# Routing the last token tile from un-normalised values, with logits corrected by mean and deviation

## The reference

```
mixed = merged @ w_out
x = LN1(alpha * x + mixed)               # (v - mean) * rsqrt(var + eps) * g + b
group = argmax(x @ w_rg)                 # 4 groups
two experts of that group by x @ w_re    # 32 experts in all
moe = sum over the two of weight * (silu(x @ w1[e]) * (x @ w3[e])) @ w2[e]
ple = sigmoid(x @ w_ple_gate) * (p @ w_ple)
x = LN2(alpha * x + moe + ple)
```

## Time and profile before

| | |
|---|---|
| runs | 1535.27, 1535.79, 1536.26 us, median 1535.79 |
| profiled execution | 1533.7 us, span 1531.9 us, mean granted clock of PE 0.932 |
| PE busy | 1288.9 us, 84% |
| DVE, ACT, POOL busy | 404.1, 284.8, 54.0 us |
| data moved | 488.77 MB, mean 319 GB/s |
| border from mixing to experts | 303 to 317 us in layer 0, 1055 to 1069 us in layer 1 |

### The profile page before, as it was taken

How to read it: one execution, slowest core, us unless ns; L and a number is a source line. 1 busy time by engine, 2 the same in 40 slices (tenths; PEclk the granted TensorE clock), 3 DMA queues, 4 the chain that set the end, 5 groups by cost and what they waited for, 6 DMA issues and landing times.

```text
span 1531.9 us, 20304 instructions
## 1 busy us (share of the span) xinstructions
PE 1288.9 (84%) x8528; PEld 718.5 (47%) x8529; DVE 404.1 (26%) x1027; ACT 284.8 (19%) x712; POOL 54.0 (4%) x94
## 2 busy tenths in 40 slices
PE   7999999999788777755799999999997786776754
PEld 4766887544332332321276678766442331332311
DVE  4142633532111101100133446245211211101003
ACT  3342422021001101000034434212111101010001
POOL 1300000000000000000022010000000000000000
PEclk9999999999898978988999999999998998888887
DMA  9503435999999999999962042579999999999994
GB/s 332 163 1 110 172 117 180 417 363 426 427 427 426 426 427 426 427 426 426 407 217 84 32 149 102 181 268 372 403 427 427 426 426 427 427 426 427 426 426 162
DMA packets 99534, 488.77 MB, mean 319 GB/s; under 512 B 9520, under 2 KB 15600, under 8 KB 51952
## 3 DMA queue, kind: packets, MB, share of 16 engines
q1 hardware_dynamic: 94976, 476.48, 76.2%
q0 software_dynamic: 4464, 10.93, 2.4%
HBM read 484.48 MB, written 2.89 MB: 318 GB/s over the span
## 4 chain that ended last, share of the span: by engine, by line
PE 58%; DMA 33%; SPq 6%; DVE 2%; issue 1%; ACT 0%; POOL 0%; DVEq 0%
PE bank L1002 55%; DMA arena<-in_w_e_up 12%; DMA arena<-in_w_e_down 8%; DMA ring<-in_w_e_down 5%; DMA arena<-in_w_e_gate 3%; SPq L791 3%; SPq L857 2%; DMA xT<-in_w_e_down 2%; PE bank L1052 2%; DMA ring<-in_w_e_gate 2%; DMA ring<-in_w_in 1%; DVE arena L2007 0%; DVE x_sb L2016 0%; PE bank L1447 0%; DVE arena L2119 0%
## 5 line engine op out<-in xcount | busy, mean ns | idle before, releaser
L1002 PE MATMUL bank<-arena 128*32 128x512 f32 (+13 forms) x2840 | 546.9, 537 | 101.5 <-DMA arena<-in_w_e_down 22.8
L1002 PE MATMUL bank<-ring,arena 128*32 128x512 f32 (+4 forms) x1248 | 398.2, 645 | 38.0 <-issue 16.0
L1002 PEld LDWEIGHTS bank<-arena 128*32 128x32 f32 (+4 forms) x2840 | 199.5, 136 | 307.2 <-issue 298.7
L1002 PE MATMUL bank<-ring,xT 128*32 128x128 f32 (+5 forms) x1536 | 236.5, 363 | 1.3 <-ACT xT L1608 1.1
L1002 PE MATMUL bank<-xT,ring 128*128 128x288 f32 x768 | 191.8, 407 | 0.0
L1002 PEld LDWEIGHTS bank<-ring,xT 128*32 128x32 f32 (+1 forms) x1536 | 121.1, 137 | 100.3 <-issue 89.6
L1002 PEld LDWEIGHTS bank<-xT,ring 128*128 128x128 f32 x768 | 143.7, 190 | 37.9
L1002 PEld LDWEIGHTS bank<-ring,arena 128*32 128x32 f32 (+1 forms) x1248 | 97.9, 130 | 107.6 <-issue 93.9
L1002 PE MATMUL bank<-arena,x_sb 128*128 128x128 f32 (+1 forms) x768 | 99.7, 282 | 1.4 <-DVE arena L2339 0.8
L1002 PEld LDWEIGHTS bank<-arena,x_sb 128*128 128x128 f32 (+1 forms) x768 | 90.5, 190 | 19.5 <-issue 12.7
L1002 PE MATMUL bank<-lb,arena 128*32 128x512 f32 x128 | 73.6, 729 | 28.3 <-DMA arena<-in_w_e_up 28.3
(11 more groups left out here) (234 smaller groups left out, 892.5 us busy)
## 6 DMA issues: line engine op xcount, KB each, us to landing
arena<-in_w_e_gate SPq DMA_DIRECT2D x76, 1024.0 KB, 25.6
arena<-in_w_e_up SPq DMA_DIRECT2D x70, 1024.0 KB, 26.2
arena<-in_w_e_down SPq DMA_DIRECT2D x60, 1024.0 KB, 26.2
ring<-in_w_e_up SPq DMA_DIRECT2D x42, 1024.0 KB, 26.3
ring<-in_w_e_gate SPq DMA_DIRECT2D x38, 1024.0 KB, 26.3
ring<-in_w_e_down SPq DMA_DIRECT2D x38, 1024.0 KB, 26.2
ring<-in_w_in SPq DMA_DIRECT2D x32, 1024.0 KB, 10.0
lb<-in_w_e_up SPq DMA_DIRECT2D x12, 1024.0 KB, 26.5
```

What stands on the lines that cost most here:

```text
L1002: return pe.matmul(out, lhsT, rhs, start=first, stop=last, skip_group_check=True)
```

## The change

Tile 1 is no longer routed from LN1's result. Its residual sums are transposed as they are (`turn_raw`, one half of the features as soon as its sum is written) and multiplied with `wr_scaled`, the router columns times LN1's g. The logits come out of three terms: with s the raw product, m the mean and r the inverse deviation of a token, they are r * (s - m * sum(g w)) + sum(b w). The two sums over features are 16 products with one-column weights (`router_sums`; g and b by columns are the new input `ln1_cols`), copied to SBUF by ACT and spread over 128 partitions by one product (`spread_sums`). LN1 of tile 1 still runs, partly beside the routing; its second half is shifted after `place_tile(1)`. The normalised tile is transposed into `xT` in quad 0, behind the choice's transposition. `plain(0, 2)` moves from the border to quad 0, behind `plain(1, 2)`. `gather_first((2, 0))` now stands behind `router(1)`.

```diff
-            (("rk", 2), 4), (("rk", 0), 5), (("wo", 1, 1), 2), (("t1", 1, 0), 0), (("t1", 1, 1), 1), (("rt", 1), 3),
-            (("pl", 0, 2), 2), (("pg", 0, 2), 5), (("rk", 1), 4), (("XT0", 0), 6), (("XT0", 1), 7), (("cnt",), 3)]
+            (("rk", 2), 4), (("rk", 0), 5), (("raw", 0), 0), (("wo", 1, 1), 2), (("sw",), 7), (("raw", 1), 1), (("sb",), 7), (("rt", 1), 3),
+            (("rk", 1), 4), (("XT0", 0), 6), (("XT0", 1), 7), (("cnt",), 3)]
...
+    turned = [(("t1", 1, 0), 5), (("t1", 1, 1), 6)]
+    j = [(("G",), 0)] + ([(("ST0",), 4)] + turned if g == 0 else [])
...
+    j += [(("Y", 0), 5), (("Y", 1), 6)] + (plain(1, 2, 1, 2) + plain(0, 2, 7, 0) if g == 0 else []) + combine
...
+        norm_cols = carve(5568, 2, 8)
+        wr_scaled = carve(5584, 8, 36)
...
                 pool.dma_start(pT[:, :, SEQ:T], p_sample[layer]).then_inc(ple_in, 16)
+                pool.dma_start(norm_cols, ln1_cols[layer].rearrange("p (k c) -> p k c", k=2)).then_inc(norm_cols_in, 16)
...
-                            job_read(pe, (layer, "t1", t, c // 4))
+                            job_read(pe, (layer, "raw", c // 4) if t == 1 else (layer, "t1", t, c // 4))
+                        ins = mm(b[0:NT[t], 0:36], xT[:, c, now(t)], (wr_scaled if t == 1 else wr)[:, c, :], c == 0, c == 7)
...
+                def turn_raw(h):
+                    pe.wait_ge(x_mixed, 2 * layer + h + 1)
+                    transposes(layer, ("raw", h), [((c % 4) * P, P, x[0:P, 1, c * P:c * P + P]) for c in range(4 * h, 4 * h + 4)])
+                def router_sums():
+                    pe.wait_ge(norm_cols_in, 16 * (layer + 1))
+                    b = open_bank((layer, "sw"))
+                    for k in range(2):
+                        for c in range(8):
+                            ins = mm(b[0:1, 36 * k:36 * k + 36], norm_cols[:, k, c:c + 1], wr[:, c, :], k + c == 0, c == 7)
+                    done(ins)
+                def spread_sums():
+                    job_read(pe, (layer, "sw"))
+                    b = open_bank((layer, "sb"))
+                    done(mm(b[:, 0:72], ones[0:1, :], wr_sums[0:1, :], True, True))
...
                 rank(0)
+                turn_raw(0)
                 half_mix(1, 1)
+                router_sums()
+                turn_raw(1)
+                spread_sums()
+                pe.wait_ge(wr_scaled_out, layer + 1)
+                router(1)
                 pe.wait_ge(sel_early, layer + 1)
                 gather_first((2, 0))
-                turn_mixed(1)
-                router(1)
                 pe.wait_ge(ple_in, 32 * (layer + 1))
-                plain(0, 2)
                 rank(1)
...
                         transpose_choice((layer, "ST0"))
+                        turn_mixed(1)
...
                         plain(1, 2)
+                        plain(0, 2)
...
+                read_raw(0)
+                act.activation(wr_sums[0:1, 0:36], bank(key)[0:1, 0:36], ACT.Copy, scale=-1.0)
+                emptied(act.copy(wr_sums[0:1, 36:72], bank(key)[0:1, 36:72]), key)
+                read_raw(1)
+                layer_norm(1 + 2 * layer, (1,))
+                emptied(act.copy(wr_sums_all, bank(key)[:, 0:72]), key)
...
+                    if t == 1:
+                        job_read(dve, (layer, "sb"))
+                        dve.wait_ge(ln_rstd, ln_place(1 + 2 * layer, t))
+                        step(dve.scalar_tensor_tensor(raw_logits, wr_sums_all[:, 0:36], mvs[:, 2:3], b[:, 0:36], ALU.mult, ALU.add))
+                        step(dve.scalar_tensor_tensor(raw_logits, raw_logits, ln_rs[:, 1:2], wr_sums_all[:, 36:72], ALU.mult, ALU.add))
...
+                dve.tensor_tensor(wr_scaled, wr, bcast(norm_cols[:, 0, :], 2, 36), ALU.mult).then_inc(wr_scaled_out, 1)
...
-                normalize(1 + 2 * layer, 1, x[:, 1, :], x_half)
-                read_x("t1", layer, xT, (1,))
+                job_done(dve, (layer, "raw", 1))
+                for h in range(2):
+                    half = x[:, 1, 512 * h:512 * h + 512]
+                    ins = dve.scalar_tensor_tensor(half, half, mvs[:, 2:3], lnw[:, 0, 512 * h:512 * h + 512], ALU.subtract, ALU.mult)
+                step(ins)
                 route_tile(1)
+                shift_half(0).then_inc(x_half, 1)
                 place_tile(1).then_inc(sel_out, 1)
+                shift_half(1).then_inc(ln_out, 1)
...
-                gated(0, 2)
...
+                        read_x("t1", layer, xT, (1,))
...
                         gated(1, 2)
+                        gated(0, 2)
```

More of the change, by code:

```diff
@@ L279, in __init__ @@
                 for job, b in expert_jobs(g):
-                    enter((layer,) + job if job[0] in ("pl", "pg", "ST0") else (layer, "moe", g) + job, b)
+                    enter((layer,) + job if job[0] in ("t1", "pl", "pg", "ST0") else (layer, "moe", g) + job, b)
     def number(self, key):
@@ L604, in build @@
         ln_rows_out = sem("ln_rows_out")
+        norm_cols_in = sem("norm_cols_in")
+        wr_scaled_out = sem("wr_scaled_out")
+        x_mixed = sem("x_mixed")
         rows_in = sem("rows_in")
@@ L1322, in router @@
                         if c % 4 == 0:
-                            job_read(pe, (layer, "t1", t, c // 4))
-                        ins = mm(b[0:NT[t], 0:36], xT[:, c, T0[t]:T0[t] + NT[t]], wr[:, c, :], c == 0, c == 7)
+                            job_read(pe, (layer, "raw", c // 4) if t == 1 else (layer, "t1", t, c // 4))
+                        ins = mm(b[0:NT[t], 0:36], xT[:, c, now(t)], (wr_scaled if t == 1 else wr)[:, c, :], c == 0, c == 7)
                     done(ins)
+                def turn_raw(h):
[12 more added lines that the diff above has]
+                    done(mm(b[:, 0:72], ones[0:1, :], wr_sums[0:1, :], True, True))
                 def turn_mixed(t):
                     for h in range(2):
[L1330 to L1333, removed]
+                        pe.wait_ge(ln_out, ln_place(2 * layer + 1, t))
                         transposes(layer, ("t1", t, h), [((c % 4) * P, P, x[0:NT[t], t, c * P:c * P + P]) for c in range(4 * h, 4 * h + 4)])
@@ L1375, in gather_first @@
                         for t in tiles:
+                            if t == 1 and h == 0:
+                                pe.wait_ge(x_half, 2 * layer + 2)
+                            elif t == 1:
+                                pe.wait_ge(ln_out, ln_place(2 * layer + 1, t))
                             for c in range(4):
@@ L1528, in _ @@
                     if g == 0:
+                        for h in range(2):
+                            job_read(pe, (layer, "t1", 1, h))
                         plain(0, 1)
@@ L1873, in plain_gate, with read_raw @@
                     emptied(act.activation(sums(layer, t, j), for_sums(layer, t, bank(key)), ACT.Sigmoid), key)
-                for t in MIX_ORDER:
-                    layer_norm(1 + 2 * layer, (t,))
-                    read_x("t1", layer, t, (0, 1) if t != 1 else (0,))
+                def read_raw(h):
+                    key = (layer, "raw", h)
+                    job_done(act, key)
+                    emptied(act.copy(xT[:, 4 * h:4 * h + 4, now(1)], transposed(bank(key), 1)), key)
+                for t in (2, 0):
+                    layer_norm(1 + 2 * layer, (t,))
+                    read_x("t1", layer, t, (0, 1))
+                read_raw(0)
+                key = (layer, "sw")
+                job_done(act, key)
+                act.activation(wr_sums[0:1, 0:36], bank(key)[0:1, 0:36], ACT.Copy, scale=-1.0)
+                emptied(act.copy(wr_sums[0:1, 36:72], bank(key)[0:1, 36:72]), key)
+                read_raw(1)
+                layer_norm(1 + 2 * layer, (1,))
+                key = (layer, "sb")
+                job_done(act, key)
+                emptied(act.copy(wr_sums_all, bank(key)[:, 0:72]), key)
                 for t in MIX_ORDER:
@@ L1940, in _ @@
                         read_choice((layer, "ST0"))
+                        read_x("t1", layer, 1, (0,))
                         plain_gate(0, 1)
@@ L1951, in _ @@
                         plain_gate(1, 2)
+                        plain_gate(0, 2)
                         read_tokens((layer, "moe", g, "XT", 0))
@@ L2320, in route_tile @@
                     step(dve.tensor_scalar(r[:, 48:52], iota[0:n, 0:4], r[:, 16:17], 2 * BIG, ALU.is_equal, ALU.mult))
[L2321 to L2324, removed]
+                    ins = dve.scalar_tensor_tensor(lg[:, 8:40].rearrange("p (g e) -> p g e", g=GROUPS), bcast(r[:, 48:52], 2, PER_GROUP),
+                                                   BIG, b[0:n, 4:36].rearrange("p (g e) -> p g e", g=GROUPS),
+                                                   ALU.subtract, ALU.min)
+                    if t == 1:
+                        step(ins)
+                    else:
+                        emptied(ins, key)
+                        job_read(dve, key)
                     step(dve.max(r[:, 24:32], lg[:, 8:40]))
@@ L2347, in place_tile @@
                     return ins
```

(18 more changed lines are left out.)

14 lines of the change are left out of this document (10 added, 4 removed).

## The result

The changed kernel takes 1542.2 us in the median of 22 runs (1530.35 to 1547.24); the kernel before takes 1535.33 beside it (22 runs, 1533.69 to 1538.27). It is slower: the medians differ by 6.9 us, the means by 5.2, because the changed kernel's runs are spread over 17 us with some short ones among them. The recorded ratio is 1.0034, with an interval of 1.0019 to 1.0049. The forecast was 1533.2, with a range of 1530.3 to 1536.0, and no rival that I named gives this time for the reason that holds.

A forecast was written before the change was run, and what follows sets the result against it. The expert weight stream was taken to bound the kernel, stalling once per layer at the mixing-to-experts border. Experts 1.3 us sooner in 2 layers save 2.6: profiled 1533.7 becomes 1531.1, median 2.1 above, 1533.2 us; range 1530.3 to 1536.0.

The forecast's parts named there:

- PE is at its higher level throughout: At the border from mixing to experts, TensorE was taken to run at granted clock 1.00, 2.4 GHz.
- so layer 0 is worked out and doubled: Layer 1 was said to run layer 0's sequence, so its 1.3 us saving was counted twice: 2.6 us.
- The sums: `router_sums` on PE after the last `wo` half: 16 matmuls, 32 records, 1.55 us, bounds 1.28 and 1.87.
- the spread row: `spread_sums` before `router(1)`: 0.35 us waiting for ACT's copy, an estimate between 0 and 0.7, plus 0.1 for the matmul.
- `gather_first`, not routing, is last: Behind `router(1)`, `gather_first((2, 0))` holds PE until 312.1, 1.0 us later than routing's 311.1.
- The two corrections: Two small DVE operations turning raw logits into logits: 0.45 us with hand-over, costing nothing because `gather_first` ends later.
- The one gap of PE: Sign of a correct forecast: between the last `wo` half and the experts, PE has no gap over 0.3 us.
- The shift's second half: LN1's second half, behind `place_tile(1)`, lasts until 314.3; the gather wants it at 314.4, late by 0.2 at worst.
- The correction costs what it saves: Rival: sums, spread row and late second half add up at the border; 1.3 us longer erases the gain, 1535.8; chance 0.13.
- a warm restart: Rival: blocks follow the `lnw` piece without a stream start-up, up to 1.5 us more a layer, 1530.2; chance 0.20.
- Quad 0 starves the stream: Rival: PE's later release in quad 0 is paid if under 2.6 us of transfers lie ahead: 1541.0; chance 0.07.
- `plain(0, 2)` leaves PE, where it stood in the shadow of routing, so its removal saves nothing: At the border, moving these products to quad 0 was priced at zero; in quad 0 they take 2.30 us.

The follow-up runs named there:

- again: The changed kernel run once more with no edit, to profile an execution of usual length: 1542.64 us, ratio 1.0053.
- plain_back: The changed kernel with `plain(0, 2)` put back at the border, ahead of `rank(1)`, new routing kept: 1544.59 us, ratio 1.006.
- move_only: The kernel before with only `plain(0, 2)` moved from the border to quad 0, LN1 and routing unchanged: 1538.97 us, ratio 1.0019.
- thick: The changed kernel plus two unread dense 512-column products, one behind `router(1)`, one behind `gather_first((2, 0))`: 1536.41 us, ratio 1.0003.
- thick_small: The changed kernel plus two unread dense products of 128 columns, behind `router(1)` and behind `gather_first((2, 0))`: 1542.83 us, ratio 1.0041.
- sums_early: The changed kernel with `router_sums` and `spread_sums` moved ahead of the mixing: 1545.14 us, ratio 1.0049.

## Why the prediction was wrong, by its own steps

The step that failed is a sentence in the first part: "PE is at its higher level throughout (granted clock 1.00, 2.4 GHz)". It is true of the kernel before, and all prices of the new chain were then taken at that level. No rival lets it change. At the lower level `gather_first((2, 0))`, `rank(1)` and the gather take 3.1, 0.7 and 1.7 us more, 5.5 a border. In an execution that loses both borders, 2 x 5.5 less the 2.6 gained makes 8.4 us; **again** shows 8.8, and the median is 6.9. That in a median execution part of a border is spared, as in the profiles of the changed kernel and of **plain_back**, is argued, since runs without a profile don't show their borders.

The doubling ("so layer 0 is worked out and doubled") failed with it: the changed kernel's own profile holds the clock in one layer and not in the other.

The steps of the border were right. The sums cost 1.13 instead of 1.55, under the lower bound of 1.28: 0.035 a record, below `router(2)`'s 0.040. `turn_raw(1)` took 0.58 for 0.42, the spread row 0.37 for 0.45, `router(1)` 1.91 for 1.86. `gather_first`, not routing, is last: `rank(1)` starts at its end, 312.18. The two corrections take 0.69 on DVE instead of 0.45, hidden as said. The one gap of PE, 0.38 ahead of the gather, is over the 0.3 that was named as a sign, but the kernel before has the same one. The shift's second half ends at 314.23 (forecast 314.3), and the gather shows no wait for it. One reading was off, without consequence: in the expert stages PE goes down to 5 tenths, not 6.

*The correction costs what it saves* and *a warm restart* did not come: in layer 0 the experts started 1.27 us sooner, and the stream lost 1.25 less. *Quad 0 starves the stream* gave the right sign for a reason that the rows refute: PE is later there (issue at 368.66, for 365.81 before: 2.85, forecast 2.6), its new wait is 0.88, and the stream stays at 424 to 428 GB/s in every 10-us window from 330 to 400.

"`plain(0, 2)` leaves PE, where it stood in the shadow of routing, so its removal saves nothing" was right of its time and blind to its second effect: **move_only** shows that the clock goes with it.

## What to carry to other kernels

In this case TensorE's granted clock went with the order of its work: a reordering of light, weight-load-bound products needs its own reading of the clock, and a chain on TensorE should be priced at both levels, with the lower one as a rival. Work that fills idle time may be holding the clock, so ask what it is worth before moving it. Where a profile is better than the median, look at the spread of the runs first, and profile again.

## What the runs showed of the hardware that was not expected

TensorE's clock fell to 0.50 with PE busy in every microsecond (**again**), and two unneeded dense products of about a microsecond each between the light ones kept it at 1.00 (1536.4 against 1542.2); with a quarter of the columns they did not.

PE stands idle between quad 7's gate and up products, where the program reads a count and branches on it, waiting for nothing that the profile shows: 8.02 us in layer 0 of the kernel before, 13.69 in the changed kernel, 8.04 in **thick** (7.7 to 8.8 in layer 1 of every kernel). The rows, from the timelines of these three kernels in this order:

```profile
730.18 1.07 PE L1002 MATMUL bank<-ring,arena 128*32 128x512 f32 x3 [8.02 <-issue]
```

```profile
735.04 1.08 PE L1012 MATMUL bank<-ring,arena 128*32 128x512 f32 x3 [13.69 <-issue]
```

```profile
732.59 1.08 PE L1012 MATMUL bank<-ring,arena 128*32 128x512 f32 x3 [8.04 <-issue]
```

It does not go with the clock of the border: 13.35 in **again**, where the clock fell, and 8.13 in **thick_small**, where it fell too. The profiles with 13.4 to 13.7 (the changed kernel's two, **plain_back**, **sums_early**) are of the same PE instructions in three orders; all kernels with a few more or fewer have 7.9 to 8.2. That the code's place decides is argued from this, not shown. In the changed kernel's first profile it costs layer 0 what the border gained: SP issues the layer's last piece 1.0 us earlier than before (738.06 for 739.07), but its last down products end 0.1 later (758.25 for 758.12), with no wait for a DMA. In **again**, an execution of the usual length, it costs nothing, as the last down products there wait for the stream:

```profile
762.91 0.63 PE L1012 MATMUL bank<-ring,arena 128*32 128x512 f32 x3 [0.79 <-DMA xT<-in_w_e_down]
```
